# More activation chunks transposed through DRAM and VectorE, and seven feature items as merged halves, in a two-block fp32 network

## What is computed

```python
# first block
u = rmsnorm(h, attn_norm_w)
z, xbc, dt_raw, q, kc, vc, ks, vs, kw, vw, gate_raw = split(u @ w_in)
mixed = concatenate([ssd_mixer(...), nsa_mixer(...)])
h = h + mixed @ w_out
v = rmsnorm(h, ffn_norm_w)
h = h + (silu(v @ w_gate) * (v @ w_up)) @ w_down      # 5632 hidden
x = rmsnorm(h, final_norm_w)
# second block
h = rms_norm(x, norm_mix_pre)
a_q, a_f, a_i, a_g, b_q, b_k, b_v, b_f, g_a, g_b = split(h @ w_in_2)
y_a = hgrn2_mixer(a_q, a_f, a_i, a_g, ...) @ w_up_a
y_b = fox_mixer(b_q, b_k, b_v, b_f + b_fox_f) @ w_up_b
x = x + rms_norm((sigmoid(g_a) * y_a + sigmoid(g_b) * y_b) @ w_o, norm_mix_post)
gate, up = split(rms_norm(x, norm_ffn_pre) @ w_ffn_in)
x = x + rms_norm((silu(gate) * up) @ w_ffn_down, norm_ffn_post)
```

## Time and profile before

| | us |
|---|---|
| median of the runs | 2614.7 |
| the profiled run | 2614.97 |
| its span on the core | 2613.2 |
| PE busy | 2601.7 (100%) |
| DVE busy | 1493.4 (57%) |
| ACT busy | 1233.0 (47%) |
| granted clock of TensorE | 0.999 |

### The profile page before, as it was taken

One profiled execution on the slowest core, in us unless ns is written; L12 is line 12 of the kernel. 1 busy time (PEld: TensorE's weight loads), 2 busy tenths in 40 slices (PEclk: granted clock), 3 DMA queues, 4 the chain that ended last, 5 costly groups with the idle time before them and its releaser, 6 DMA issues.

```text
span 2613.2 us, 33053 instructions
## 1 busy us (share of the span) xinstructions
PE 2601.7 (100%) x13542; PEld 2222.8 (85%) x13542; DVE 1493.4 (57%) x1790; ACT 1233.0 (47%) x1561; POOL 0.2 (0%) x4
## 2 busy tenths in 40 slices
PE   9999999999999999999999999999999999999998
PEld 9999788888888888899899888888888888888887
DVE  6687665555455545566567654556655545555556
ACT  5575545444444344465444454444554444443443
POOL 0000000000000000000000000000000000000000
PEclk9999999999999999999999999999999999999999
DMA  8544446665666566556544445566576666666664
GB/s 309 167 129 145 153 145 205 220 214 190 194 219 216 193 193 217 194 181 214 186 156 151 151 132 186 184 240 184 173 234 211 202 194 207 217 202 193 206 211 145
DMA packets 151751, 500.74 MB, mean 192 GB/s; under 512 B 15984, under 2 KB 32624, under 8 KB 150544
## 3 DMA queue, kind: packets, MB, share of 16 engines
q1 hardware_dynamic: 151456, 498.48, 58.9%
q10 hardware_dynamic: 144, 0.15, 0.0%
HBM read 485.59 MB, written 12.58 MB: 191 GB/s over the span
## 4 chain that ended last, share of the span: by engine, by line
PE 97%; DMA 1%; DVE 1%; ACT 0%; issue 0%; SPq 0%; DVEq 0%; ACTq 0%
PE ps L421 95%; PE ps L425 2%; DMA W<-blocks 1%; DVE wlo L1504 0%; ACT whi L996 0%; DMA scr<-in_xT 0%; DVE W L1791 0%; DMA blocks<-W 0%; SPq L2370 0%; ACT W L996 0%; DVE h L1507 0%; SPq L2326 0%; DVE W L1931 0%; DVE scr L1504 0%; DVE W L1504 0%
## 5 line engine op out<-in xcount | busy, mean ns | idle before, releaser
L1504 DVE TENSOR_TENSOR wlo<-raw,whi 128x1024 fp32r<-128x1024 f32 x886 | 1077.8, 1223 | 949.4 <-ACT whi L996 946.4
L996 ACT ACTIVATE whi<-raw 128x1024 fp32r<-128x1024 f32 x886 | 931.5, 1057 | 1091.8 <-PE ps L421 1078.7
L421 PE MATMUL ps<-whi,xlo 128*128 128x512 f32 x2080 | 815.0, 392 | 0.0
L421 PE MATMUL ps<-wlo,xhi 128*128 128x512 f32 x2080 | 810.2, 390 | 1.4 <-DVE wlo L1504 1.3
L421 PE MATMUL ps<-whi,xhi 128*128 128x512 f32 x2080 | 809.6, 389 | 0.0
L421 PEld LDWEIGHTS ps<-wlo,xhi 128*128 128x128 f32 x2080 | 390.4, 188 | 84.7 <-DVE wlo L1504 3.3
L421 PEld LDWEIGHTS ps<-whi,xhi 128*128 128x128 f32 x2080 | 390.6, 188 | 80.5 <-issue 0.5
L421 PEld LDWEIGHTS ps<-whi,xlo 128*128 128x128 f32 x2080 | 390.6, 188 | 80.3 <-issue 1.0
L421 PE MATMUL ps<-whi,hlo 128*128 128x512 f32 x944 | 370.5, 392 | 0.0
L421 PE MATMUL ps<-wlo,hhi 128*128 128x512 f32 x944 | 367.5, 389 | 0.0
L421 PE MATMUL ps<-whi,hhi 128*128 128x512 f32 x944 | 367.3, 389 | 0.0
(11 more groups left out here) (133 smaller groups left out, 998.4 us busy)
## 6 DMA issues: line engine op xcount, KB each, us to landing
raw<-in_gu SPq DMA_DIRECT2D x352, 512.0 KB, 4.2
raw<-in_w_in SPq DMA_DIRECT2D x256, 512.0 KB, 3.5
raw<-in_dn SPq DMA_DIRECT2D x176, 512.0 KB, 3.5
raw<-in_w_out SPq DMA_DIRECT2D x32, 512.0 KB, 3.5
raw<-in_w_up SPq DMA_DIRECT2D x32, 512.0 KB, 4.2
raw<-in_w_o SPq DMA_DIRECT2D x32, 512.0 KB, 3.5
blocks<-W SPq DMA_DIRECT2D x64, 128.0 KB, 3.4
W<-blocks SPq DMA_DIRECT2D x16, 512.0 KB, 5.6
```

What stands on the lines that cost most here:

```text
L421: return e.matmul(o, l, r, start=start, stop=stop, skip_group_check=skip)
L996: return e.activation(o, i, f, **kw)
L1504: return e.tensor_tensor(o, a, b, op)
```

## The change

Four things are changed, in all engines' lists alike.

1. Fifteen more chunks are bounced instead of turned on PE: the outputs of `1os0` to `1os2` (as input of the ffn), the hidden chunks of `1fu3`, `1fu7`, `2fu3`, `2fu7`, the outputs of `1fd2_0` to `1fd2_2` (input of the second block), two chunks `o0`, `o1` of the hgrn2 mixer's output, and the merged chunks of `2ub0` to `2ub2`. Thirty-one are bounced then. PE keeps the last chunk of each kind (`1os3`, `1fu10`, `1fd2_3`, `2fu10`, `2ub3`) and the fox mixer's half of the o tiles.
2. The way through DRAM is cut differently: one DMA writes the chunk as it is (end+1), four DMAs bring it back in pieces of 512 bytes (end+3), in two alternating DRAM buffers. The DVE transpose stands at the end of step end+6 (end+5 for `1fd2_2`), two steps later than before. For a hidden or merged chunk ACT's high part is in the same step and DVE's low part in the next; for `1os` and `1fd2` chunks, which are scaled by a norm's weights, ACT writes four tiles a step later. Since the pieces come back in another order of features, the rows of the weights are reordered on the host (`by_blocks`) at more places.
3. `ffn_names` puts the gate item of the next group's first chunk ahead of a group's four down items.
4. Seven feature items (`HALVES`) become two items of four units each, with 256 weight columns by four k tiles in a piece. `xhi` and `xlo` now lie side by side in `xx`, so that one matmul streams both: per k tile and 128 weight columns one matmul of 512 columns (`whi` by `[xhi|xlo]`) and one of 256 (`wlo` by `xhi`). The two products lie in different halves of a bank; at the end of a half ACT copies the second (`second`), DVE adds the first and multiplies by the norm's factor (`half`).

```diff
+HALVES = ["1q1", "2aq0", "2aq1", "2bq0", "2bq1", "2bk0", "2bk1"]
...
+        if name in HALVES:
+            fours = [list(range(k, k + 4)) for k in range(0, KT, 4)]
+            item(name + "-", src[0:4], "half", fours, 256)
+            item(name, src[4:8], "half", fours, 256)
...
+def ffn_names(b):
+    for g, (c0, c1) in enumerate(GROUPS):
+        for c in range(c0, c1):
+            if c == 0 or c > c0:
+                yield f"{b}fg{c}"
+            yield f"{b}fu{c}"
+        if c1 < NCH:
+            yield f"{b}fg{c1}"
+        for c in range(4):
+            yield f"{b}fd{g}_{c}"
...
-        xhi = sb("xhi", [P, KT, T], R)
-        xlo = sb("xlo", [P, KT, T], R)
+        xx = sb("xx", [P, KT, 2, T], R)
+        xhi, xlo = xx[:, :, 0, :], xx[:, :, 1, :]
...
+        chunks = {}
+        for n in range(3):
+            chunks[f"1os{n}"] = (len(chunks), end[f"1os{n}"], ev[f"1os{n}"], h[:, :, n * 512:n * 512 + 512])
+        for c in range(NCH - 1):
+            chunks[f"1fu{c}"] = (len(chunks), end[f"1fu{c}"], ev[f"1fu{c}"], Hb)
...
+            chunks[f"o{n}"] = (len(chunks), end["2bf"] + 8 + 8 * n, (s_oa, 2), scr[:, :, n * 512:n * 512 + 512])
+            chunks[f"2ub{n}"] = (len(chunks), end[f"2ub{n}"], (s_mg, n + 1), scr[:, :, n * 512:n * 512 + 512])
...
         PE, unit():
+                    elif it["kind"] == "half":
+                        for ct in range(2):
+                            w0 = ct * 128
+                            mm(banks[ct], wh[:, kk, w0:w0 + 128], xx[:, k, :, :].rearrange("p a b -> p (a b)"), start=a, stop=False, skip=True)
+                        on.wait_ge(s_lo, q + 1)
+                        for ct in range(2):
+                            w0 = ct * 128
+                            m = mm(banks[ct][:, 0:256], wl[:, kk, w0:w0 + 128], hi_t[:, k, :], start=False, stop=z, skip=True)
...
         ACT:
+                if it["kind"] == "half":
+                    x = halves_at.index(nm)
+                    on.wait_ge(s_unit, end[nm])
+                    if x:
+                        on.wait_ge(*ev[halves_at[x - 1]])
+                    i = items.index(it)
+                    act(second(nm), ps[:, 2 * (i % 2):2 * (i % 2) + 2, 256:512]).then_inc(s_second, 1)
...
+            def blocks_hi(nm, wcol=None):
+                yield from later(6 if nm == "1fd2_2" else 7)
+                k = tile_of(nm)
+                on.wait_ge(s_bt2, chunks[nm][0] + 1)
+                if wcol is None:
+                    act(hhi[:, k:k + 4, :].rearrange("p k (ta c) -> p k ta c", c=32), by_tiles(Ht)).then_inc(s_hhi, 4)
+                else:
+                    for j in range(4):
+                        act(xhi[:, k + j, :].rearrange("p (ta c) -> p ta c", c=32), by_tiles(Ht)[:, j], scale=wcol(k + j)).then_inc(s_xhi, 1)
...
         DVE:
-            def bounced(nm):
-                yield from later(5)
...
+            def half(nm, it):
+                own.up(tt(o, ps[:, 2 * (i % 2):2 * (i % 2) + 2, 0:256], second(nm), ADD))
+                mine()
...
+                    tt(o, o, RB2, MUL).then_inc(ev[nm][0], 1)
...
+            def blocks_lo(nm, wcol=None):
+                yield from later(6 if nm == "1fd2_2" else 7)
+                on.wait_ge(s_hlo, tiles["h"])
+                on.wait_ge(s_xlo, tiles["x"])
+                blocks_T(nm, Ht)
+                k = tile_of(nm)
+                if wcol is None:
+                    tiles["h"] += 4
+                    yield
+                    on.wait_ge(s_hhi, tiles["h"])
+                    tt(hlo[:, k:k + 4, :].rearrange("p k (ta c) -> p k ta c", c=32), by_tiles(Ht),
+                       hhi[:, k:k + 4, :].rearrange("p k (ta c) -> p k ta c", c=32).bitcast(F), SUB).then_inc(s_hlo, 4)
...
         SP, extra():
+                if g in leaves:
+                    x, _, ready, src = leaves[g]
+                    on.wait_ge(*ready)
+                    if x >= 2:
+                        on.wait_ge(s_br, 64 * (x - 1))
+                    e.dma_start(blocks[x % 2].rearrange("t p f -> p t f"), src).then_inc(s_bw, 16)
+                if g in returns:
+                    x = returns[g][0]
+                    on.wait_ge(s_bw, 16 * (x + 1))
+                    if x:
+                        on.wait_ge(s_bt2, x)
+                    for q in range(4):
+                        e.dma_start(Hs[32 * q:32 * q + 32].rearrange("c (b x) -> c b x", x=128),
+                                    blocks[x % 2].rearrange("t (a c) (q x) -> q c (t a) x", a=4, q=4)[q]).then_inc(s_br, 16)
...
-                elif g - 1 in bounced_at:
...
-                    for a in range(4):
-                        e.dma_start(blocks.rearrange("(q c) (t a x) -> a c t q x", q=4, t=2, a=4)[a],
-                                    Hb[32 * a:32 * a + 32].rearrange("c t (q x) -> c t q x", q=4)).then_inc(s_bw, 16)
-                elif g - 3 in bounced_at:
...
-                    e.dma_start(Hs, blocks).then_inc(s_br, 16)
```

More of the change, by code:

```diff
@@ L368, in ahead, with second @@
             return g + NSPL - 1 + (max(0, (g - turn + 9) // 2) if g <= turn else 0)
+        halves_at = [nm for nm in parted(HALVES, first)]
+        def second(nm):
+            return W_(18512 if nm[0] == "1" else 0, 2, T)
         def pair_of(i):
@@ L555, in walk @@
             def walk(names, side=None):
-                for nm in names:
+                for nm in parted(names, first):
                     i = at[0]
@@ L944, in o_tiles @@
             def o_tiles():
-                for k in range(0, 16, 2):
-                    tiles_T("x", XF["o"] + k, k * 128, scr, (s_oa, 2) if k < 8 else (s_fin, 12))
+                yield from later(4)
+                for k in range(8, 16, 2):
+                    tiles_T("x", XF["o"] + k, k * 128, scr, (s_fin, 12))
                     yield
@@ L1401, in o_tiles @@
                     if k < 8:
-                        tiles_hi("x", k, lambda kk: C("hnw"))
+                        on.wait_ge(s_bt2, chunks["o1"][0] + 1)
+                        on.wait_ge(s_unit, first["2gb3"] + k // 2 + 1)
+                        for kk in (k, k + 1):
+                            act(xhi[:, kk, :].rearrange("p (ta c) -> p ta c", c=32), by_tiles(Hto[kk // 4])[:, kk % 4],
+                                scale=C("hnw")[:, kk % 4:kk % 4 + 1]).then_inc(s_xhi, 1)
                     else:
@@ L1810, in start_side, with blocks_o, pairs_T @@
+            def blocks_o(n, wait):
+                yield from later(wait)
+                blocks_T(f"o{n}", Hto[n])
+            def pairs_T(wait, k):
+                yield from later(wait)
+                tiles_lo("h", k)
+                tiles_lo("h", k + 2)
             def start_side():
@@ L2336, in rotated @@
                     e.dma_start(dst[p0:p0 + 8], src[q0:q0 + 8]).then_inc(landed, 16)
-            bounced_at = {end[nm]: nm for nm in n_bounced}
+            leaves = {c[1] + 1: c for c in chunks.values()}
+            returns = {c[1] + 3: c for c in chunks.values()}
             def extra(g):
+                if g in leaves:
[12 more added lines that the diff above has]
+                                    blocks[x % 2].rearrange("t (a c) (q x) -> q c (t a) x", a=4, q=4)[q]).then_inc(s_br, 16)
                 if g == 2:
@@ L2457, in pack, with by_halves, by_blocks @@
     return np.ascontiguousarray(w.reshape(k // 256, 2, 128, chunks, CH).transpose(3, 0, 2, 1, 4)).reshape(chunks, k // 256, 128, 2 * CH)
-def by_blocks(w):
-    w = w.reshape(NCH, 4, 4, 32, D).copy()
-    for c in BOUNCED:
+def by_halves(packed, names, first):
+    for n, nm in enumerate(names):
+        if first + nm in HALVES:
+            w = packed[n].reshape(8, 128, 2, CH).transpose(0, 2, 1, 3).reshape(4, 4, 128, 2, 256)
+            packed[n] = w.transpose(3, 0, 2, 1, 4).reshape(8, 128, 1024)
+    return packed
+def by_blocks(w, chunks):
+    n = w.shape[0] // CH
+    w = w.reshape(n, 4, 4, 32, -1).copy()
+    for c in chunks:
         w[c] = w[c].transpose(1, 0, 2, 3)
-    return w.reshape(FF, D)
+    return w.reshape(n * CH, -1)
 def narrow(w):
```

219 lines of the change are left out of this document (113 added, 106 removed).

## The result

The changed kernel takes 2602.6 us (median of 4 runs, 2600.56 to 2606.08) against 2614.42 before (median of 4 runs); the ratio is 0.9953, 95% interval 0.9936 to 0.997. Forecast were 2598.1 and a range of 2592 to 2604.5: the direction and the range held, but 11.8 us were gained where 16.6 were forecast.

What follows compares the result with a forecast made beforehand. TensorE's instruction stream was taken as the bound (busy 2601.7 of 2613.2 us). Transposes -13.5, halves -6.0, old stalls -3.0 and new stalls +5.9 gave -16.6, so 2598.1 us; range 2592 to 2604.5 (8 in 10).

Steps and rivals of the forecast that it cites:

- Transposes: PE: thirteen chunks lose eight transposes each, 0.89 us a chunk, and four o-tile groups lose four, 0.49 each; -13.5 us.
- Old stalls: PE's waits for `wlo` and late weight loads go, as the transpose comes two steps later; -3.0 us, ends 0 and 3.3.
- Halves: Seven feature items, 56 units: merged 512-column matmuls make each unit 0.106 us shorter; -6.0 us, or 0 at worst.
- The term of 2aq0: At 2aq0: shorter units and each half's DVE `add` and `mul` make `wlo` late; +1.0 us, between nothing and 2.1.
- 1fg0: 1os2 to 1fg0: four `xhi` and four `xlo` ACTIVATEs against a margin of one unit; +0.5 us, ends 0 and 3.
- 2af0: At 2af0's fifth unit: ACT gets 1.57 and DVE 1.25 us more against 2.2 of slack; +0.7 us, ends 0 and 2.9.
- 2ub2 to 2o0: At 2o0's fifth unit: `hlo` of 2ub2's chunk comes late and PE waits; +3.7 us, ends 2.9 and 6.
- Rival E: Near consumers of 2ub2 and 1os2 stall by their upper ends, 6 + 3 us; -11.8, 2602.9 us; chance 0.08.
- Rival B: DVE's free time absorbs all new stalls but 2ub2's 2.9 us; -19.6, 2595.1 us; chance 0.13.
- rival D: The halves gain nothing, the two-part operand or extra evictions eating 6.0 us; -10.6, 2604.1 us; chance 0.13.

Runs made afterwards that it cites:

- fu_early: The changed kernel with the up items' chunks transposed two steps earlier, at end+4; 2620.89 us, ratio 1.0021 to the kernel before.
- the early return: The changed kernel with 2ub2's write and return each one step earlier and chunks leaving in two writes of 256 KB; 2600.61 us.
- the outlier: Profiled run, 2601.01 us (median 2595.94), of the changed kernel with 2ub2's write one step earlier, transpose and `hhi` at end+5, `hlo` right behind `hhi`.
- the early write: The changed kernel with only the write of 2ub2's chunk issued one step earlier (end+0); 2600.49 us.
- the filled stand: The changed kernel with sixteen extra PE matmuls of 512 columns ahead of the wait at 2o0's fifth unit; 2600.44 us. `fill16` is the same run.
- no_halves: The changed kernel with `HALVES` empty, all 15 chunks and the order kept; 2607.14 us.

## Why the prediction was right, and where it was not

- **Transposes:** 0.89 a chunk and 0.49 a group of four, 13.5 in all, measured 13.5.
- **Old stalls:** -3.0 forecast, -2.9 measured. The reason given, that the transpose finds its data two steps later, is borne out by `fu_early`, where the same new way through DRAM with the transpose two steps earlier brings more stalls than there were. The old way with the later transpose was not run.
- **Halves:** -6.0 forecast, -5.2 measured, which is the mechanism with its size a little off. (The fixed time per matmul that the prediction gives as 13.6 ns is 13.2 to 13.5 by its own rows 6 and 8; its sum does not use it.) The term of 2aq0 was forecast at 1.0 and came out at 0.5.
- **1fg0:** 0.5 forecast, 1.0 measured, the wait being 0.70 for `xx` (the low part), as described. **2af0:** 0.7 forecast; 1.0 in the profile of after, 0 in three of the others and up to 4.4 (7.1 where the high parts were moved), so this term is not one number, and its cause is not the forecast one (more work on ACT and DVE). It follows DVE's wait for the return of 1fd2_2's chunk, whose transpose stands a step earlier than the others: 1.06 us of waiting and 1.0 of stall in the profile of after, 1.97 and 1.9 with the early return, 2.57 and 3.9 in the outlier, where the clock fell too, and no stall in the three profiles without a wait. That 0.7 was near to 1.0 is luck.
- **2ub2 to 2o0**, the step that failed: 3.7 forecast, 7.25 measured, because of two things.
  The first is the wait itself. It came out as forecast (3.75, in another profile 5.51) by luck, since two sizes were wrong in opposite senses. The prediction counts from ACT's start on the step of the transpose, which is here

```profile
1781.14 1.06 ACT L1065 ACTIVATE whi<-raw 128x1024 fp32r<-128x1024 f32 x1 [1.66 <-PE ps L484]
```

  It let the transpose start 2.3 us behind it, as in a plain stretch, or 3.1 with its 0.8 for the evictions. The transpose really started 4.6 us behind it, and 0.34 of that was the wait for the return; with the early write, without any such wait, it was 4.05 (1780.10 to 1784.15). DVE was still at the eviction and merging of 2ub3, at the low part of 2ub1's chunk, which the sum had left out, and at the splits behind them, 8.3 us without a gap. So `hlo` was done after 10.4 us, not after 8.9. On the other side PE stood from 1787.91, 6.8 us behind ACT's start, and not from 5.2: two units lie between, as counted, but also the eight transposes of 2ub3, which stay on PE and were left out; they took 1.4 us here. DVE is busy 17.46 of 20 us there (1766 to 1786 in the profile after) where it had been 14.87 in the same window before, which lies in the ub stretch too; the 57% of the page say nothing of it.
  The second is what remains of the 7.25, 3.5 us, which was priced at nothing: 2.7 us for thirteen steps while the clock was at its lower level, 0.5 at 2ub3's transposes (1.4 us for 0.89; PE reached them when DVE had only just ended the merging), and 0.3 in the steps around the stand. That a stand of PE costs more than its length is shown by the filled stand (-2.2 us with `hlo` as late).
- The wrong term carries 3.5 of the 4.8 us that are missing (16.6 forecast, 11.8 measured) and the halves 0.8; the rest, half a microsecond, is the sum of the small terms.
- Rival E had the right place and a price of 6 for it, and its total of 2602.9 is close to the measured time, partly by luck: it put all evictions into the chain, knew nothing of the slow steps, and gave 1os2 3 us where 1.0 was measured. Rival B is refuted by the waits at 1fg0 and 2o0, rival D by `no_halves`.

Not settled: why the return's landing varies by 2 us and more from run to run at 2ub2 and 2af0; no run here isolates it.

## What to carry to other kernels

When work moves from a full engine to a half-empty one, ask in which stretch it lands: count the receiver's busy time and the work's place in its queue there, unit by unit, and count what the consuming engine itself still has to do before it needs the result. A chunk whose consumer is near is better left where it was; one such chunk of fifteen cost 6.7 us, more than half of what the whole change gained. A stand of TensorE of some microseconds has to be priced with the slow steps that follow it.

## What the runs showed of the hardware

- The granted clock fell from 1.00 to 0.50 in or just behind every single stand of PE of 2.65 us and longer, in a kernel whose PE is otherwise hardly ever idle; in the two profiles of the changed kernel 13 and 7 steps of 512 columns were slow behind it, most of them 0.427 in place of 0.227 us. Behind a single 1.43 us (`fill16`) and 1.53 us (the run with the high parts in the transpose's step) it stayed up, but it fell behind two waits close together, 1.21 and 0.76 us, and 1.61 and 0.76 us, at 2af0. The longer of the two stands (5.51 against 3.75) had the fewer slow steps (7 against 13).
- A 512 KB write to DRAM with 2-KB rows took 6.3 to 6.6 us to land in the profile of after (5.2 to 5.8 in that of the early write), four of 128 KB with 512-byte pieces 3.4 each before, two of 256 KB 4.5 to 5.0, while weight loads of 512 KB took 3.4 to 4.4.
- DVE's transpose of 128x1024 fp32 took 1.24 or 1.25 us wherever it is shown, against 0.89 us of PE time for the same tiles.
